# Moving the sums of ACT's partial products in a depthwise convolution from VectorE to GpSimd

## The chip, the cores and the metric

The kernel runs on one NeuronCore of a Trainium2 chip. The metric is the device time of one execution in microseconds, given as the median of several runs. A profile is taken of one further execution.

The engines are called by their names or by the short names of the profile: TensorE (PE, and PEld for its weight loads), VectorE (DVE), ScalarE (ACT), GpSimd (POOL) and SyncE (SP).

## The reference

A decoder trunk of two layers over 256 tokens of 2048 features, all in float32. Layer 0 mixes tokens with a Conformer convolution module, layer 1 with differential attention. Each layer goes on with a gated feed-forward part (5632 hidden features, a depthwise convolution of width 3) and a gated per-layer embedding. The change touches only the first mixer, of which this is the core:

```python
def conformer_conv(x, w_pw1, b_pw1, w_dw, b_dw, ln_g, ln_b, w_pw2, b_pw2):
    a, g = jnp.split(x @ w_pw1 + b_pw1, 2, axis=-1)
    u = a * jax.nn.sigmoid(g)
    u = causal_dwconv(u, w_dw) + b_dw          # 31 taps for each feature
    u = jax.nn.silu(layer_norm(u, ln_g, ln_b))
    return u @ w_pw2 + b_pw2
```

## The kernel before

**Tiling.** Features lie on the 128 partitions, so the 2048 features are 16 feature tiles, and the 256 tokens are the columns. The first mixer works on one feature tile at a time (the code counts `p` from 0 to 15, `PAIRS` is 16). All engines run their own instruction streams, written out by hand; they meet only at counting semaphores.

**What each engine does for a tile p of the first mixer.**

- TensorE computes two blocks of `x @ w_pw1` into PSUM, the value block and the gate block of the tile (`glu_unit`, matmul at L1783). It may run up to four tiles ahead of VectorE, since it has PSUM banks for two chunks of two tiles.
- ACT computes the sigmoid of the gate block (`gate_of`, L747). VectorE multiplies it with the value block into `u_ext` (`gated`, L1213). `u_ext` holds 30 columns of zeros and then the 256 tokens, so that a tap is a shifted view of it.
- The 31 taps are shared out. ACT takes taps 0 to 9 (`first_taps`, L768, `ACT_PAIRS` is 5): the first two begin the accumulators `acc2` (from the third tile on ACT does only tap 0 of these and VectorE tap 1), the other eight are written as four products `products[:, 0..3]`, each with two halves of 256 columns, 512 columns in all. VectorE takes taps 10 to 30 (`convolve`, L1237), each a multiply-add into one of the two halves of `acc2`. For the last tile TensorE takes the last 14 taps as matmuls with diagonal matrices (`tap_diag`, L1876), and VectorE only eight.
- The four products must become one. In `convolve`, VectorE adds `products[:, 1]`, `[:, 2]` and `[:, 3]` onto `products[:, 0]`, three sums of 128x512, spread between its taps (L1248). Each waits for its product (`products_made`) and for the sum before it (`products_added`). `join` (L1255) adds the result to `acc2`, and L1261 adds its two halves into `vq`. ACT squares that (L755), and `add_up` (L1224) keeps the running sum over tiles for the layer norm.

`join(p)` is not called at once but behind `gated(p + 1)`, so that ACT can start the next tile's taps early. ACT may overwrite a product of the tile before only when `products_added` has counted the sum that read it.

**Behind the last tile.** TensorE takes the token means of the values and the squares, VectorE centres, scales and splits them, GpSimd computes a reciprocal root on two columns (`power`, L566), and the second pointwise matmul begins. From there on the kernel streams weights: SP loads blocks of 256 KB, ACT rounds each into `w_hi`, VectorE computes the remainder `w_lo`, and TensorE multiplies with both.

**GpSimd** makes constants, issues a few DMAs and computes the reciprocal roots. Its queue in the first mixer holds `load_gain` and `load_bias` (two DMAs, at 42 us), and then the root of the layer norm.

Of the kernel before, what the change touches and what calls it, by code (L numbers as in the profile page):

```python
# [24 lines left out]
ALU = mybir.AluOpType  # L25
# [42 lines left out]
def trunk(nc, t, out):  # L68
# [20 lines left out]
    ACT_PAIRS = 5  # L89
# [5 lines left out]
    PAIRS = 2 * CH_GLU  # L95
# [107 lines left out]
    def tenant(at, name, shape, dt=F32):  # L203
        assert at % 32 == 0
        return nc.alloc_sbuf_tensor_at(name, shape, dt, offset=at)
# [23 lines left out]
    products = tenant(arena + 16 * SLOT, "products", [P, ACT_PAIRS - 1, 2, T])  # L229
# [35 lines left out]
    with ctx:  # L265
        def sem(name):
            return ctx.enter_context(nc.semaphore(name))
# [46 lines left out]
        products_made = sem("products_made")  # L314
        products_added = sem("products_added")
# [107 lines left out]
        def load_constants(engine, which):  # L423

            n = 0
            for g, (parts, _, _, _) in enumerate(groups):
                row = 0
                for _, src in parts:
                    if consts_loader(n) == which:
                        engine.dma_start(const_rows[row:row + src.shape[0], g], src).then_inc(consts_landed[which], 16)  # L430
                    row += src.shape[0]
                    n += 1
# [113 lines left out]
        def _(pool):  # L546
# [15 lines left out]
            def power(dst, src, n):  # L562

                powers[0] += 1
                pool.wait_ge(var_ready, powers[0])
                nc.gpsimd.tensor_tensor(dst, src, minus_half[:, 0:n], ALU.pow).then_inc(rstd_ready, 1)  # L566
# [5 lines left out]
            def load_bias(src):  # L572
                pool.dma_start(bias[:], src.partition_broadcast(P)).then_inc(bias_landed, 16)
# [4 lines left out]
            load_gain(t["post_mix_g"][0])  # L578
            pool.wait_ge(cols_turned, len(groups))
            load_bias(t["conv_b_pw2"][0])  # L580
            power(rstd[:], meansq[:], HALVES)
            pool.wait_ge(early_ready, EARLY[0])
            pool.dma_start(z_saved[0][:], z_early[:]).then_inc(early_stored, 16)
# [41 lines left out]
        def _(act):  # L625
# [92 lines left out]
            def keep_columns(some):  # L718
                for g in some:
                    _, rows, of, first = groups[g]  # L720
                    act.wait_ge(cols_turned, g + 1 if g < 2 else len(groups))
                    dst = {"cols": cols, "conv": wconv}[of]
                    bank, at = column_bank(g)
                    nc.scalar.copy(dst[:, first:first + rows], ps[:, bank, at:at + rows]).then_inc(cols_ready, 1)
# [307 lines left out]
        def _(dve):  # L1032
# [183 lines left out]
            def add_up(p):  # L1216

                if 1 <= p < SUMMED:
                    dve.wait_ge(squared, p + 1)
                    if p == SUMMED - 1:  # L1220
                        dve.wait_ge(v_done, p + 1)
                    if p > 1:
                        dve.wait_ge(v_summed, p - 1)
                    nc.vector.tensor_tensor(vq_sum[:], vq[:, p], vq[:, 0] if p == 1 else vq_sum[:], ALU.add).then_inc(v_summed, 1)  # L1224

            def convolve(p, taps):

                both, sums = acc2[:, p % 2], products[:, 0]
                dve.wait_ge(glu_done, p + 1)
                dve.wait_ge(accs_begun, p + 1)  # L1230
                made = [None, None]
                each = len(taps) // (ACT_PAIRS - 1)
                for n, tap in enumerate(taps):
                    a = n % 2
                    if made[a] is not None:
                        dve.wait_ge(dve_step, made[a])
                    step.mark(nc.vector.scalar_tensor_tensor(both[:, a], u_ext[:, p, tap:tap + T],  # L1237
                                                             wconv[:, tap * KT + p:tap * KT + p + 1],
                                                             nshift[:] if tap == 1 else both[:, a], ALU.mult, ALU.add))
                    made[a] = step.value()  # L1240
                    if p == PAIRS - 2 and n == len(taps) // 2:
                        add_up(p - 1)
                    k = (n + 1) // each
                    if (n + 1) % each == 0 and 1 <= k < ACT_PAIRS - 1:
                        dve.wait_ge(products_made, (ACT_PAIRS - 1) * p + k + 1)
                        if k > 1:
                            dve.wait_ge(products_added, (ACT_PAIRS - 1) * p + k - 1)
                        nc.vector.tensor_tensor(sums, sums, products[:, k], ALU.add).then_inc(products_added, 1)  # L1248
                dve.wait_ge(dve_step, step.value())
                dve.wait_ge(products_added, (ACT_PAIRS - 1) * p + ACT_PAIRS - 2)  # L1250
# [12 lines left out]
            for p in range(PAIRS):  # L1263
                if p == 1:
                    unscaled(1)
                gated(p)
                if p:
                    join(p - 1)
                if p == 2:
                    dve.wait_ge(shift_ready, 1)  # L1270
                    dve.wait_ge(v_done, 2)
                    nc.vector.tensor_tensor(vq[:, 0:2, 0], vq[:, 0:2, 0], nshift[:].unsqueeze(1).to_broadcast([P, 2, T]),
                                            ALU.add).then_inc(v_shifted, 1)
                if 3 <= p < PAIRS - 1:
                    add_up(p - 2)
                taps = list(range(2 * ACT_PAIRS, CK - (PE_TAPS if p == PAIRS - 1 else 0)))
                convolve(p, taps if p < 2 else taps[0:1] + [1] + taps[1:])
                if p == PAIRS - 3:
                    split(None, 0, 0, 1)
# [87 lines left out]
            for layer in range(DEPTH):  # L1367
                if layer == 1:
# [83 lines left out]
                    for a in range(STEPS):  # L1452
# [7 lines left out]
                        c, k = divmod(a - PV_LAG - 1, BPC)  # L1460
# [627 lines left out]
```

## Time and profile before

| | us |
|---|---|
| median of 3 runs | 2421.08 |
| lowest and highest run | 2413.65, 2421.11 |
| the profiled execution | 2422.17 |
| its span | 2420.4 |
| TensorE busy | 2410.6 (100%) |
| VectorE busy | 1640.4 (68%) |
| ACT busy | 1239.0 (51%) |
| GpSimd busy | 36.2 (1%) |

The span runs from the first to the last recorded instruction; 1.8 us of the profiled execution lie outside it. Busy shares are means over the whole span, and a busy TensorE is not TensorE at its peak, because matmuls overlap and their ends are modelled. A float32 matmul leaves two records. The first mixer ends near 346 us; its convolution, of which the change is a part, lies between 35 and 246 us.

### The profile page before, as it was taken

The page shows a single profiled execution, that of the slowest core. Times are in us where ns is not written, and L with a number is a line of the kernel's source. Part 1 is how long each engine was busy: PE and PEld are TensorE (multiplying, and loading weights), DVE is VectorE, ACT ScalarE, POOL GpSimd, SP SyncE. Part 2 cuts the span into 40 slices and gives each one's busy share as a digit, 9 for nine tenths or more (in the row PEclk, how much of TensorE's full clock was granted, in tenths as well). Part 3 has the DMA queues.
Part 4 walks back from the last instruction along what each step waited for, and adds up shares of the span by engine and source line. Part 5 has one row for each costly group of instructions (what it writes and reads, how often), then busy time and mean ns, then how long its engine had stood idle before and what let it go on. Part 6 is the DMA issues. An engine that isn't in the chain of part 4 may idle for free.

```text
span 2420.4 us, 38834 instructions
## 1 busy us (share of the span) xinstructions
PE 2410.6 (100%) x12378; PEld 2058.2 (85%) x12378; DVE 1640.4 (68%) x2231; ACT 1239.0 (51%) x1777; POOL 36.2 (1%) x66
## 2 busy tenths in 40 slices
PE   9999999999999999999999999999999999999999
PEld 8888788888888888888888888888888888888887
DVE  6999767777777754447655677577777777644475
ACT  3433655555555544446644455466655656544464
POOL 2000000000000000000000000000000000000000
PEclk9999999999999999999999999999999999999999
DMA  8552546656656565556566544645566566655564
GB/s 265 180 166 92 174 157 197 183 180 193 184 177 198 183 211 193 195 193 221 193 202 206 182 157 150 196 157 182 184 199 190 182 191 194 210 193 194 193 231 150
DMA packets 370942, 452.48 MB, mean 187 GB/s; under 512 B 27460, under 2 KB 279494, under 8 KB 369440
## 3 DMA queue, kind: packets, MB, share of 16 engines
q1 hardware_dynamic: 367456, 435.54, 56.5%
q0 software_dynamic: 2960, 15.02, 1.8%
q8 instruction: 44, 0.72, 0.1%
q10 hardware_dynamic: 432, 0.79, 0.1%
q14 instruction: 50, 0.41, 0.1%
HBM read 447.05 MB, written 4.19 MB: 186 GB/s over the span
## 4 chain that ended last, share of the span: by engine, by line
PE 98%; SPq 0%; DVE 0%; issue 0%; DMA 0%; ACT 0%; POOL 0%; DVEq 0%; POOLq 0%; ACTq 0%
PE ps L1701 32%; PE ps L1703 16%; PE ps L1728 13%; PE ps L1730 13%; PE ps L1729 13%; PE ps L1783 9%; PE ps L1673 1%; PE ps L1949 0%; PE ps L1935 0%; SPq L477 0%; DMA h<-in_x 0%; PE ps L1876 0%; PE ps L1790 0%; PE ps L1884 0%; PE ps L1657 0%
## 5 line engine op out<-in xcount | busy, mean ns | idle before, releaser
L1044 DVE TENSOR_TENSOR w_lo<-raw,w_hi 128x1024 fp32r<-128x1024 f32 x758 | 923.8, 1224 | 631.8 <-ACT w_hi L634 625.7
L1701 PE MATMUL ps<-x,w_hi 128*128 128x512 f32 x3328 | 1165.5, 396 | 1.3 <-DVE w_lo L1044 1.3
L634 ACT CAST w_hi<-raw 128x1024 fp32r<-128x1024 f32 x758 | 791.4, 1049 | 727.7 <-PE ps L1730 361.8
L1703 PE MATMUL ps<-x,w_lo 128*128 128x256 f32 x3328 | 928.7, 279 | 0.0
L1701 PEld LDWEIGHTS ps<-x,w_hi 128*128 128x128 f32 x3328 | 624.4, 188 | 149.3 <-DVE w_lo L1044 1.8
L1703 PEld LDWEIGHTS ps<-x,w_lo 128*128 128x128 f32 x3328 | 627.1, 188 | 0.0
L1728 PE MATMUL ps<-w_hi,mid 128*128 128x512 f32 x704 | 273.9, 389 | 0.0
L1729 PE MATMUL ps<-w_lo,mid 128*128 128x512 f32 x704 | 273.9, 389 | 0.0
L1730 PE MATMUL ps<-w_hi,mid 128*128 128x512 f32 x704 | 273.9, 389 | 0.0
L1728 PE MATMUL ps<-w_hi,x 128*128 128x512 f32 x640 | 253.2, 396 | 0.0
L1730 PE MATMUL ps<-w_hi,x 128*128 128x512 f32 x640 | 249.2, 389 | 0.0
L1729 PE MATMUL ps<-w_lo,x 128*128 128x512 f32 x640 | 249.2, 389 | 0.0
L1783 PE MATMUL ps<-xn,wg 128*128 128x256 f32 x896 | 193.7, 379 | 0.0
L1783 PEld LDWEIGHTS ps<-xn,wg 128*128 128x128 f32 x896 | 170.2, 190 | 23.1
L1505 DVE SCALAR_TENSOR_TENSOR acc<-ext,cols,acc 128x256 f32<-128x256 f32 x352 | 147.2, 480 | 46.0 <-ACT acc L951 39.6
L1728 PEld LDWEIGHTS ps<-w_hi,mid 128*128 128x128 f32 x704 | 132.2, 188 | 27.5
L1730 PEld LDWEIGHTS ps<-w_hi,mid 128*128 128x128 f32 x704 | 132.2, 188 | 27.4
L1729 PEld LDWEIGHTS ps<-w_lo,mid 128*128 128x128 f32 x704 | 132.2, 188 | 27.4
L1730 PEld LDWEIGHTS ps<-w_hi,x 128*128 128x128 f32 x640 | 120.1, 188 | 25.4
L1728 PEld LDWEIGHTS ps<-w_hi,x 128*128 128x128 f32 x640 | 120.2, 188 | 24.8 <-issue 0.4
L1729 PEld LDWEIGHTS ps<-w_lo,x 128*128 128x128 f32 x640 | 120.2, 188 | 24.6 <-issue 0.2
L1237 DVE SCALAR_TENSOR_TENSOR acc<-u_ext,wconv,acc 128x256 f32<-128x256 f32 x322 | 134.1, 482 | 1.2 <-ACT acc L768 1.1
(202 smaller groups left out, 1310.4 us busy)
## 6 DMA issues: line engine op xcount, KB each, us to landing
raw<-in_ffn_w_in SPq DMA_DIRECT2D x704, 256.0 KB, 3.1
raw<-in_ffn_w_out SPq DMA_DIRECT2D x352, 256.0 KB, 3.5
raw<-in_attn_w_qkv SPq DMA_DIRECT2D x192, 256.0 KB, 2.9
raw<-in_ple_w_gate SPq DMA_DIRECT2D x128, 256.0 KB, 3.6
wg<-in_conv_w_pw SPq DMA_DIRECT2D x112, 256.0 KB, 4.0
raw<-in_conv_w_pw SPq DMA_DIRECT2D x64, 256.0 KB, 3.6
raw<-in_attn_w_o SPq DMA_DIRECT2D x64, 256.0 KB, 3.5
wg<-in_conv_w_pw SPq DMA_DIRECT2D x32, 128.0 KB, 4.0
```

The lines of the kernel that those rows point to most:

```text
L634: nc.scalar.copy(w_hi[:, u % RING], raw[:, u % RING]).then_inc(hi_split, 1)
L1044: nc.vector.tensor_tensor(w_lo[:, u % RING], raw[:, u % RING], w_hi[:, u % RING].bitcast(F32), ALU.subtract).then_inc(split_done, 1)
L1237: step.mark(nc.vector.scalar_tensor_tensor(both[:, a], u_ext[:, p, tap:tap + T], wconv[:, tap * KT + p:tap * KT + p + 1], nshift[:] if tap ...
L1505: ins = nc.vector.scalar_tensor_tensor(acc[:, f], ext[:, f, tap:tap + T], col(f"ffn_tap{layer}{tap}", c * 2 + (f if f < 2 else FT + f - 2) ...
L1673: ins = nc.tensor.transpose(tiles[:, turned_at(left, kt), P * half:P * (half + 1)], h[:, half, P * kt:P * (kt + 1)], ident[:])
L1701: mm(ps[:, 4 * s + f], w_hi[:, u % RING, q, columns], x[:, kt].rearrange("p a t -> p (a t)"), start=kt == 0, stop=False)
L1703: ins = mm(ps[:, 4 * s + f, 0:T], w_lo[:, u % RING, q, columns], x[:, kt, 0], start=False, stop=kt == KT - 1)
L1728: mm(bank(half), hi, w_hi[:, u % RING, q], start=first, stop=False)
L1729: mm(bank(half), hi, w_lo[:, u % RING, q], start=False, stop=False)
L1730: ins = mm(bank(half), lo, w_hi[:, u % RING, q], start=False, stop=last)
L1783: ins = mm(ps[:, 4 * (c % 2) + f, 0:T], wg[:, glu_slot(u), q, P * f:P * (f + 1)], source[:, kt], start=kt == 0, stop=kt == KT - 1)
```

## The change

The three sums of products for tiles 0 to 14 are written into GpSimd's stream, ahead of the root of the layer norm, with the same semaphores. VectorE keeps only those of tile 15. Its wait for the third sum at the end of `convolve` (`products_added` at 4p + 3) stays, and is now a wait for GpSimd. The sum is the same operation on the same columns: 128x512 float32, written in place onto `products[:, 0]`.

```diff
@@ -578,6 +578,12 @@
             load_gain(t["post_mix_g"][0])
             pool.wait_ge(cols_turned, len(groups))
             load_bias(t["conv_b_pw2"][0])
+            for p in range(PAIRS - 1):
+                for k in range(1, ACT_PAIRS - 1):
+                    pool.wait_ge(products_made, (ACT_PAIRS - 1) * p + k + 1)
+                    if k > 1:
+                        pool.wait_ge(products_added, (ACT_PAIRS - 1) * p + k - 1)
+                    nc.gpsimd.tensor_tensor(products[:, 0], products[:, 0], products[:, k], ALU.add).then_inc(products_added, 1)
             power(rstd[:], meansq[:], HALVES)
             pool.wait_ge(early_ready, EARLY[0])
             pool.dma_start(z_saved[0][:], z_early[:]).then_inc(early_stored, 16)
@@ -1241,7 +1247,7 @@
                     if p == PAIRS - 2 and n == len(taps) // 2:
                         add_up(p - 1)
                     k = (n + 1) // each
-                    if (n + 1) % each == 0 and 1 <= k < ACT_PAIRS - 1:
+                    if p == PAIRS - 1 and (n + 1) % each == 0 and 1 <= k < ACT_PAIRS - 1:
                         dve.wait_ge(products_made, (ACT_PAIRS - 1) * p + k + 1)
                         if k > 1:
                             dve.wait_ge(products_added, (ACT_PAIRS - 1) * p + k - 1)
```

VectorE's order for the fourth tile (p = 3) before, from its gated product to the next one. A name's number tells apart buffers of one name, and x5 means five in a row:

```order
L1213 SCALAR_TENSOR_TENSOR u_ext<-ps,cols,glu_gate 128x256
L1255 TENSOR_TENSOR acc_94<-acc_94,products 128x512
L1261 TENSOR_TENSOR vq<-acc_94 128x256
L1224 TENSOR_TENSOR vq_sum<-vq 128x512
L1237 SCALAR_TENSOR_TENSOR acc_94<-u_ext,wconv,acc_94 128x256
L1237 SCALAR_TENSOR_TENSOR acc_94<-u_ext,wconv,nshift 128x256
L1237 SCALAR_TENSOR_TENSOR acc_94<-u_ext,wconv,acc_94 128x256 x3
L1248 TENSOR_TENSOR products<-products 128x512
L1237 SCALAR_TENSOR_TENSOR acc_94<-u_ext,wconv,acc_94 128x256 x5
L1248 TENSOR_TENSOR products<-products 128x512
L1237 SCALAR_TENSOR_TENSOR acc_94<-u_ext,wconv,acc_94 128x256 x5
L1248 TENSOR_TENSOR products<-products 128x512
```

The same tile in the changed kernel, whose lines lie six further down:

```order
L1219 SCALAR_TENSOR_TENSOR u_ext<-ps,cols,glu_gate 128x256
L1261 TENSOR_TENSOR acc_94<-acc_94,products 128x512
L1267 TENSOR_TENSOR vq<-acc_94 128x256
L1230 TENSOR_TENSOR vq_sum<-vq 128x512
L1243 SCALAR_TENSOR_TENSOR acc_94<-u_ext,wconv,acc_94 128x256
L1243 SCALAR_TENSOR_TENSOR acc_94<-u_ext,wconv,nshift 128x256
L1243 SCALAR_TENSOR_TENSOR acc_94<-u_ext,wconv,acc_94 128x256 x20
```

The three sums between the taps are gone, and the taps stand in one row of 22. GpSimd's queue in the first mixer in the changed kernel, from the first root to the store behind the second:

```order
L566 TENSOR_TENSOR rstd<-meansq,minus_half 128x2
L570 DMA gain<-in_post_mix_g 128x2048
L573 DMA bias<-in_conv_b_pw 128x2048
L586 TENSOR_TENSOR products<-products 128x512 x45
L566 TENSOR_TENSOR rstd<-meansq,minus_half 128x2
L589 DMA z_saved<-z_early 128x2048
```

The row with x45 is new, three sums for each of 15 tiles; the other rows stand there as before. The streams of TensorE, ACT and SP are the same in both kernels.

## Rows read from the trace of the kernel before

**Rows 1.** The page: TensorE's busy time (first line), and the chain that ended last

```profile
PE 2410.6 (100%) x12378; PEld 2058.2 (85%) x12378; DVE 1640.4 (68%) x2231; ACT 1239.0 (51%) x1777; POOL 36.2 (1%) x66
...
PE 98%; SPq 0%; DVE 0%; issue 0%; DMA 0%; ACT 0%; POOL 0%; DVEq 0%; POOLq 0%; ACTq 0%
```

**Rows 2.** Busy us of PE, PEld, DVE, ACT, POOL; clock; DMA, by window

```profile
50.50:235.50 185.00, 185.00 (x859) 162.86 (x858) 175.28 (x403) 69.59 (x168) 0.00 (x0) 1.00 0.48 153
```

**Rows 3.** Timeline of VectorE: start us, us, engine, line, operation [idle before <-releaser]

```profile
98.56 0.48 DVE L1213 SCALAR_TENSOR_TENSOR u_ext<-ps,cols,glu_gate 128x256 f32<-128x256 f32 x1
...
102.60 0.69 DVE L1248 TENSOR_TENSOR products<-products 128x512 f32<-128x512 f32 x1
103.20 2.06 DVE L1237 SCALAR_TENSOR_TENSOR acc<-u_ext,wconv,acc 128x256 f32<-128x256 f32 x5
...
112.15 0.48 DVE L1213 SCALAR_TENSOR_TENSOR u_ext<-ps,cols,glu_gate 128x256 f32<-128x256 f32 x1 [0.93 <-ACT glu_gate L747]
```

**Rows 4.** Timeline of ACT: a tile's products, and the gates of the last two tiles

```profile
99.67 3.30 ACT L768 ACTIVATE products<-u_ext,wconv 128x256 f32<-128x256 f32 x8
...
222.05 0.47 ACT L747 ACTIVATE glu_gate<-ps,cols 128x256 f32<-128x256 f32 x1 [7.55 <-PE ps L1783]
...
235.87 0.47 ACT L747 ACTIVATE glu_gate<-ps,cols 128x256 f32<-128x256 f32 x1 [8.46 <-PE ps L1783]
```

**Rows 5.** VectorE's waits, 50 to 237 us: us, times, longest; and the last of them

```profile
DVE u_ext L1213 <- ACT glu_gate L747: 9.5, 9, 1.2
...
236.47 0.48 DVE L1213 SCALAR_TENSOR_TENSOR u_ext<-ps,cols,glu_gate 128x256 f32<-128x256 f32 x1 [0.53 <-ACT glu_gate L747]
```

**Rows 6.** Timeline of the last tile: TensorE's diagonal taps, and VectorE's use of them

```profile
237.01 5.02 PE L1876 MATMUL ps<-u_ext,tap_diag 128*128 128x256 f32 x22
...
243.10 1.54 PE L1876 MATMUL ps<-u_ext,tap_diag 128*128 128x256 f32 x6
...
244.75 0.42 DVE L1259 TENSOR_TENSOR acc<-ps,acc 128x256 f32<-128x256 f32 x1 [0.43 <-PE ps L1876]
```

**Rows 7.** Timeline of GpSimd, around the layer norm of the first mixer

```profile
247.85 0.72 POOL L566 TENSOR_TENSOR rstd<-meansq,minus_half 128x2 f32<-128x2 f32 x1 [204.42 <-DVE meansq L1310]
```

**Rows 8.** Groups of GpSimd instructions: busy us, mean ns of one, idle before

```profile
L597 POOL TENSOR_SCALAR_AFFINE_SELECT mask<-mask 128x128 f32<-128x128 f32 x1 | 0.5, 484 | 0.1
L594 POOL MEMSET mask<- 128x256 f32 x1 | 0.3, 332 | 0.0
...
L551 POOL MEMSET minus_half<- 128x16 f32 x1 | 0.1, 109 | 0.0
```

**Rows 9.** Timeline and groups: GpSimd instructions that overlap with VectorE's

```profile
1189.21 0.69 DVE L1083 TENSOR_TENSOR z<-z,gain 128x512 f32<-128x512 f32 x1
1189.39 1.06 POOL L566 TENSOR_TENSOR rstd<-meansq,minus_half 128x2 f32<-128x2 f32 x1 [75.30 <-DVE meansq L1062]
...
1482.39 1.01 POOL L566 TENSOR_TENSOR orstd<-omean,minus_half 128x4 f32<-128x4 f32 x1 [13.04 <-DVE omean L1440]
1482.44 1.23 DVE L1044 TENSOR_TENSOR w_lo<-raw,w_hi 128x1024 fp32r<-128x1024 f32 x1
...
1577.63 0.68 DVE L1085 TENSOR_TENSOR y_mix<-ps,gain 128x512 f32<-128x512 f32 x1
1577.80 0.70 POOL L566 TENSOR_TENSOR rstd<-meansq,minus_half 128x2 f32<-128x2 f32 x1 [85.74 <-DVE meansq L1062]
...
L566 POOL TENSOR_TENSOR orstd<-omean,minus_half 128x4 f32<-128x4 f32 x4 | 4.1, 1015 | 216.3 <-DVE omean L1440 216.3
```

**Rows 10.** Timeline of the first tile's end: VectorE's result, TensorE's load of it

```profile
49.52 0.42 DVE L1261 TENSOR_TENSOR vq<-acc 128x256 f32<-128x256 f32 x1
50.27 0.41 PEld L1838 LDWEIGHTS ps<-vq,inv_p 128*128 128x128 f32 x2
```

**Rows 11.** Timeline of TensorE: one small matmul at the program's start and later

```profile
1.54 2.93 PE L1790 MATMUL ps<-ident 128*128 128x128 f32 x12 [1.54 <-POOL minus_half L551]
...
347.40 1.06 PE L1790 MATMUL ps<-ident 128*128 128x128 f32 x8
```

## The prediction

> **What bounds the kernel now.** I read the page first: TensorE is busy for 2410.6 us of the 2420.4 us span, and the chain that ended last is 98% TensorE [rows 1]. So a saving on another engine is worth nothing unless TensorE waits for it, and a delay costs only where TensorE comes to wait.
>
> The change lies in the first mixer, so I next took the busy time of each engine in that stretch [rows 2]: from 50.5 to 235.5 us TensorE has 185.0 of 185.0 us at a granted clock of 1.00 (2.4 GHz), VectorE 175.28 us, GpSimd none. TensorE's pairs of matmul blocks (one feature tile each) set the pace, and VectorE, which convolves one tile per pair, follows with little to spare.
>
> How little is read in VectorE's timeline [rows 3]. The gated product of one tile starts at 98.56 us, the next at 112.15 us after 0.93 us of idling for ACT's gate. So a tile is 12.66 to 12.7 us of VectorE work, against 13.82 us between two gates, which is TensorE's pair (235.87 less 222.05) [rows 4]. The waits of the stretch sum it up: VectorE waited for a gate nine times, 9.5 us in all, the last time directly before the last tile, at 236.47 us [rows 5]. This **9.5 us is VectorE's whole reserve**. The first of the nine is at 112.15 us: until then it was behind TensorE. Work added beyond the reserve moves the last tile's start, one for one. Work taken away only lengthens the waits, since the last gate comes from TensorE at 235.87 us whatever VectorE does.
>
> What hangs on that start: TensorE's 14 diagonal taps of the last tile begin at 237.01 us, when the gated product is there, and VectorE adds their sum at 244.75 us before the normalization can begin [rows 6]. From there to the end the chain is TensorE's own, and nothing behind gives time back.
>
> **The change part by part.** *Removed from VectorE*: 45 sums over 128x512 (three for each of 15 tiles). One takes 0.69 us, but the next instruction starts 0.60 us behind it (102.60 to 103.20) [rows 3]. This is 45 x 0.60 = 27.0 us. By itself it is worth nothing at the end: the cover that hides VectorE, TensorE's own 185 us, is already the longer.
>
> *Added on GpSimd*: 45 sums of the same shape. The queue there is empty for 204 us before 247.85 us, where the reciprocal root of the normalization comes [rows 7]; both DMAs in the queue lie before that. ACT has a tile's products ready at 102.97 us (99.67 + 3.30), 4.4 us behind the start of the gated product, and VectorE wants the sum only behind its 22 taps, at 111.2 us (112.15 - 0.93) [rows 3, 4], so even three sums of 1.7 us are done in time and the new wait for them at the end of a tile is empty, if GpSimd may read when it likes. ACT overwrites a product only in the next tile, before which it idles for 8.46 us [rows 4].
>
> *Price of one GpSimd sum.* The trace has none of this size. The nearest rows [rows 8]: a memset of 16 columns took 109 ns and one of 256 columns 332 ns, so 0.93 ns for each column written and 0.09 us fixed; an affine select over 128 columns, which reads too, took 484 ns, 3.0 ns a column. With one pass of 512 columns at the memset's rate the low end is 0.57 us, at the select's rate the high end 1.6 us. I take two passes, one for each operand, at the memset's rate: 2 x 512 x 0.93 ns + 0.09 = 1.04 us. The memsets are the plainer work, while the select has to compare as well.
> By the Trainium skill (GPSIMD Engine Reference, 3.1 Elementwise — side-by-side cycle accounting) such an addition over 2048 columns takes 4497 ns, because both operands pass one read port; a quarter would be 1.12 us, an estimate from that page, and the sum below would end 3.6 us higher by it.
>
> *What that does to VectorE.* Here is the step on which everything rests. At 1189.39 us GpSimd's small root began while VectorE ran a product of two SBUF operands (z and gain, until 1189.90), and took 1.06 us. The same instruction at 1577.80 us, beside a product of which one operand is in PSUM, took 0.70 us [rows 9]. The 0.36 us more is about what was left of VectorE's instruction: the two do not read SBUF together. All 22 taps and the sums of a tile have two SBUF operands. So I expect the taps and the GpSimd sums to run one after the other, and each GpSimd sum to hold VectorE for its length, 1.04 us, where VectorE's own cost it 0.60.
> Against it stand 1482.39 and 1482.44 us [rows 9]: GpSimd began first, VectorE's two-operand subtraction right behind, and neither was longer than usual (1.01 us beside a mean of 1.015 over four such roots; 1.23 us for 1024 columns is no more than twice the 0.69 us of 512). I put this down to the size: four columns are read at once.
> The Trainium skill (SBUF — State Buffer, Who interferes with whom) gives whoever starts first the shared ports for the whole instruction, and by that the subtraction should have ended 0.9 us late. The trace does not agree in that pair, and agrees at 1189 us.
>
> *The sum.* Held for h per sum, VectorE gets 45 x (h - 0.60) more work, of which 9.5 us is absorbed. With h = 1.04: 19.8 - 9.5 = **10.3 us**. Check by tiles: 12.68 + 3 x 0.44 = 14.0 us a tile, above the 13.82 us of a pair, and at 98.56 us VectorE is late already, since it waits only a tile later; so VectorE never catches up and all of its waits go. The first tile also delays TensorE, whose means of that tile are loaded at 50.27 us, 0.33 us after VectorE's sum [rows 10]; that runs beside VectorE's own lag and adds nothing. TensorE itself, which may be four pairs ahead, goes on to 235.7 us and then stands.
>
> *Clock.* It will stand in two pieces of some 4 to 6 us, before the sum of squares and before the taps. At the program's start, after no work, 12 small matmul records took 2.93 us, 0.24 each; the same form later took 1.06 us for 8, so 0.13 or less each [rows 11], though the granted clock reads 1.00 in both. If the first ran at 1.2 instead of 2.4 GHz, the loss there was about 1.4 to 1.6 us. The taps and what follows are on the path, so I add 1.6 us. The ends are 0 and 6.6 us (all 28 tap records, 5.02 + 1.54 us, at half speed) [rows 6].
> The Trainium skill (TensorE: Matmul & The Clock Gate, Part 1) has the array fall to the lower level after idling, which no row of this trace shows inside the program.
>
> Total: 10.3 + 1.6 = 11.9 us. The profiled execution took 2422.2 us, so 2434.1; the median of the runs, 2421.1, lies 1.1 us below it: **2433.0 us**, 0.5% slower. About 0.3%, or 7.3 us, is what a measurement of this kernel can tell from no change.
>
> **The rivals.** *R1, no slower: the sums run beside the taps.* If GpSimd takes only gaps between VectorE's instructions, or h stays at or below 0.81 us (9.5 / 45 + 0.60, the point where the reserve is used up), the last gated product stays at 236.47 us and the time at 2421 us. For it: the undisturbed pair at 1482 us, and the low end of 0.57 us. Against it: 1189 us. Up to h = 0.97 the result is still within 0.3%, without the clock term. Chance 0.29.
>
> *R2, much slower.* If a sum holds VectorE for the 1.6 us of the select's rate, or if GpSimd is kept out while taps follow each other and does its three sums when VectorE has stopped, with a handover each, the addition is up to 45 x 1.0 - 9.5 = 35.5 us, with the clock 37: 2458 us. The middle of such cases is near 2445 us. For it: the taps start every 0.4 us and last 0.48, so there may be no gap at all. Against it: the root at 1189 us got in as soon as one instruction of VectorE ended. Chance 0.12.
>
> *R3, faster: VectorE's 27 us come off the path.* This wants TensorE to wait for VectorE in the stretch; it shows no idle time there [rows 2], and the 0.33 us at 50 us is on the good side. Chance 0.04. That the change doesn't do what it says I leave at nothing: the order of the instructions shows the 45 sums moved.
>
> **How the numbers follow.** The forecast, h from about 0.95 to 1.2 us, has 0.55 and its own range from 2427 to 2440 us (45 x 0.35 - 9.5 = 6.3; 45 x 0.60 - 9.5 = 17.5, with up to 1.6 more). Slower by over 0.3% is the forecast and R2: 0.67. Within it is R1: 0.29. Faster: 0.04. A range that holds 8 in 10 must take in R1, so it begins at 2420 us, and it ends at 2445 us, which leaves out half of R2 and R3.
>
> **What would show it.** Right: GpSimd has 45 instructions of 128x512 of over 1 us between 37 and 245 us; taps that follow a start of one are stretched or late by up to a microsecond; VectorE's waits for the gate are gone after 112 us; the last gated product comes near 247 us in place of 236.47; TensorE idles from 236 us; from the normalization on, each stage is as long as before. The clock term is right if the 22 tap records take over 5.02 us. Wrong: taps every 0.40 us beside a running GpSimd sum and longer waits for the gate (R1), or a wait of VectorE for GpSimd at the end of each tile (R2).

## The result, and the profile after

| | before | after |
|---|---|---|
| median of 20 runs each, us | 2417.18 | 2434.34 |
| lowest and highest | 2412.05, 2430.95 | 2424.83, 2443.98 |
| the profiled execution | 2422.17 | 2443.98 |
| its span | 2420.4 | 2442.2 |
| VectorE busy | 1640.4 | 1655.4 |
| GpSimd busy | 36.2 | 98.4 |

The change makes the kernel slower: the ratio is 1.0059, with a 95% interval from 1.0044 to 1.0073. The prediction was 2433.0 us against 2421.1.

The runs of either kernel stand on steps 9 us apart: before near 2412, 2421 and 2431 us, after near 2425, 2434 and 2443. Step by step the difference is about 13 us. Half of the twenty runs before lie at or below 2413.65 us and the next is at 2420.71, so the median of 2417.18 stands between two steps, where no run is. The two profiled executions stand on different steps, so their difference, 21.8 us, is not the price of the change. GpSimd's timeline shows both parts. First the three marks of the kernel before (start us, us, engine, line, operation, idle before): the root of the layer norm has its row ahead of the prediction [rows 7], at 247.85 us, and these are the two loads of a gain behind the large matmul stages of the two feed-forward parts.

```profile
863.40 0.55 POOL L570 DMA_DIRECT2D gain<-in_post_ffn_g  x1 [494.06 <-DVE mid L1527]
...
2089.10 0.60 POOL L570 DMA_DIRECT2D gain<-in_post_ffn_g  x1 [492.06 <-DVE mid L1527]
```

The same in the changed kernel:

```profile
260.91 0.72 POOL L566 TENSOR_TENSOR rstd<-meansq,minus_half 128x2 f32<-128x2 f32 x1 [21.38 <-DVE meansq L1316]
...
876.36 0.56 POOL L570 DMA_DIRECT2D gain<-in_post_ffn_g  x1 [494.05 <-DVE mid L1533]
...
2110.86 0.60 POOL L570 DMA_DIRECT2D gain<-in_post_ffn_g  x1 [501.00 <-DVE mid L1533]
```

At the root the changed kernel is 13.06 us late, at 876 us 12.96 us. Then the wait in front of the last row is 501.00 us in place of 492.06, and the distance is 21.76. The waits in front of these two rows took 485.1 or 494.1 us, and 492.1 or 501.0 us, in the profiles of all the kernels shown here, in any combination, with or without work on GpSimd in the first mixer. This is a variation of the large stages, not of the change. So **the start of the variance instruction that precedes the root (247.61 us before, 260.67 us after) is the measure used below.** Behind it, the distance between the two profiles changes by 0.1 us up to each of these rows, but for these stages.

The start of the program varies too. The first gated product of the mixer, which lies ahead of everything that the change touches, starts 0.42 us earlier in the profile of the changed kernel; before and after:

```profile
35.20 0.48 DVE L1213 SCALAR_TENSOR_TENSOR u_ext<-glu,cols,glu_gate 128x256 f32<-128x256 f32 x1 [0.54 <-ACT glu_gate L747]
...
34.78 0.49 DVE L1219 SCALAR_TENSOR_TENSOR u_ext<-glu,cols,glu_gate 128x256 f32<-128x256 f32 x1 [0.55 <-ACT glu_gate L753]
```

Counted from there, the changed kernel is 13.48 us late at the variance instruction, not 13.06.

Where this time lies is shown by the busy times of the changed kernel (columns as in [rows 2]):

```profile
50.50:235.50 185.00, 183.23 (x849) 161.35 (x850) 183.80 (x344) 69.57 (x169) 53.13 (x40) 1.00 0.47 152
235.50:255.00 19.50, 12.56 (x44) 10.35 (x43) 18.51 (x36) 6.17 (x15) 3.74 (x3) 0.74 0.01 2
```

VectorE has 59 instructions fewer than in [rows 2], yet is busy for 183.80 us in place of 175.28. In the second stretch TensorE works for 12.56 of 19.50 us and its granted clock is 0.74 on average. The chain that ended last, 98% TensorE before [rows 1], now goes through VectorE for 8%:

```profile
PE 90%; DVE 8%; issue 1%; SPq 0%; DMA 0%; POOL 0%; ACT 0%; DVEq 0%; POOLq 0%; ACTq 0%
```

How a GpSimd sum meets the taps is seen in the timeline of VectorE and GpSimd in one tile:

```profile
108.61 0.48 DVE L1243 SCALAR_TENSOR_TENSOR acc<-u_ext,wconv,acc 128x256 f32<-128x256 f32 x1
108.66 1.56 POOL L586 TENSOR_TENSOR products<-products 128x512 f32<-128x512 f32 x1 [9.55 <-ACT products L774]
109.00 1.50 DVE L1243 SCALAR_TENSOR_TENSOR acc<-u_ext,wconv,acc 128x256 f32<-128x256 f32 x1
110.36 1.26 POOL L586 TENSOR_TENSOR products<-products 128x512 f32<-128x512 f32 x1
110.42 1.48 DVE L1243 SCALAR_TENSOR_TENSOR acc<-u_ext,wconv,acc 128x256 f32<-128x256 f32 x1
111.83 0.47 DVE L1243 SCALAR_TENSOR_TENSOR acc<-u_ext,wconv,acc 128x256 f32<-128x256 f32 x1
```

The first sum comes 0.05 us behind the start of a tap, and takes 1.56 us in place of 1.27: it waits for that tap. The tap after it lasts 1.50 us in place of 0.48. So it goes with each sum: one tap is 1.02 us late, and the next starts 1.42 us behind it in place of 0.40. VectorE's own sum cost it 0.60 us.

The first tile is another matter. Its sums could begin only behind GpSimd's two DMAs, the first of which waits for TensorE; the timeline of GpSimd and VectorE:

```profile
41.89 0.59 POOL L570 DMA_DIRECT2D gain<-in_post_mix_g  x1 [18.67 <-PE ps L1789]
42.48 0.53 POOL L573 DMA_DIRECT2D bias<-in_conv_b_pw  x1
43.03 5.71 POOL L586 TENSOR_TENSOR products<-products 128x512 f32<-128x512 f32 x3
49.25 0.76 DVE L1202 TENSOR_TENSOR glu<-ps,rstd_all 128x256 f32<-128x256 f32 x2 [4.44 <-issue]
```

VectorE has finished the tile's taps at 44.8 us and idles for 4.44 us for the third sum. The second gated product comes at 50.58 us, where it came at 48.40; counted from the first one it is 2.60 us late.

The last tile, as in [rows 5, 6]:

```profile
246.78 0.48 DVE L1219 SCALAR_TENSOR_TENSOR u_ext<-ps,cols,glu_gate 128x256 f32<-128x256 f32 x1
247.32 7.77 PE L1882 MATMUL ps<-u_ext,tap_diag 128*128 128x256 f32 x22 [1.70 <-DVE u_ext L1219]
256.17 1.54 PE L1882 MATMUL ps<-u_ext,tap_diag 128*128 128x256 f32 x6
257.82 0.42 DVE L1265 TENSOR_TENSOR acc<-ps,acc 128x256 f32<-128x256 f32 x1 [3.19 <-PE ps L1882]
```

The gated product is 10.31 us late by the two profiles, 10.73 us counted from the first one, without a wait in front of it. The 22 tap records take 7.77 us in place of 5.02, which is 2.75 us. 10.73 + 2.75 = 13.48: the whole shift.

### The profile page after: what moved, and what is told of

Same layout as the page of the kernel before. It is cut to its first block, busy times and chain, and to the rows that moved or that the text cites. A ratio compares the mean times of both kernels' runs of the same rounds, so it can differ in the third digit from the quotient of the medians.

```text
span 2442.2 us, 38834 instructions
## 1 busy us (share of the span) xinstructions
PE 2423.7 (99%) x12378; PEld 2065.3 (85%) x12378; DVE 1655.4 (68%) x2186; ACT 1237.8 (51%) x1777; POOL 98.4 (4%) x111
## 4 chain that ended last, share of the span: by engine, by line
PE 90%; DVE 8%; issue 1%; SPq 0%; DMA 0%; POOL 0%; ACT 0%; DVEq 0%; POOLq 0%; ACTq 0%
PE ps L1707 32%; PE ps L1709 16%; PE ps L1734 13%; PE ps L1735 13%; PE ps L1736 13%; DVE acc L1243 7%; PE ps L1789 1%; PE ps L1679 1%; PE ps L1955 0%; PE ps L1941 0%; PE ps L1882 0%; DVE vq_sum L1230 0%; DVE acc L1261 0%; SPq L477 0%; DVE u_ext L1219 0%
## 5 line engine op out<-in xcount | busy, mean ns | idle before, releaser
L1243 DVE SCALAR_TENSOR_TENSOR acc<-u_ext,wconv,acc 128x256 f32<-128x256 f32 x322 | 172.9, 606 | 1.2 <-ACT acc L774 1.1
L1735 PEld LDWEIGHTS ps<-w_lo,mid 128*128 128x128 f32 x704 | 132.1, 188 | 27.2
```

The source lines that it names most:

```text
L1735: mm(bank(half), hi, w_lo[:, u % RING, q], start=False, stop=False)
```

## The experiments

Theory A is the prediction's: a GpSimd instruction that reads SBUF keeps VectorE's two-operand instructions from reading meanwhile, and what exceeds VectorE's reserve of 9.5 us moves the last tile. The rivals: any GpSimd activity does it (B), the loss comes from the new waits between engines (C), VectorE's sums were on the path (D). "The marker" is the variance instruction. The start of the program differs by up to 1.2 us from one profile to another, as the first gated product of the mixer shows; so the two columns of "later" count from there, and compare with the kernel before. All times are in us.

| kernel | first gated product | last gated product | marker | last, later by | marker, later by | 22 tap records |
|---|---|---|---|---|---|---|
| before | 35.20 | 236.47 | 247.61 | | | 5.02 |
| the change | 34.78 | 246.78 | 260.67 | 10.73 | 13.48 | 7.77 |
| only writing | 34.77 | 236.04 | 247.18 | 0.00 | 0.00 | 5.02 |
| one operand read | 34.02 | 241.59 | 255.22 | 6.30 | 8.79 | 7.51 |
| two operands, apart | 34.45 | 272.89 | 286.26 | 37.17 | 39.40 | 7.25 |
| half the columns | 34.42 | 248.53 | 261.96 | 12.84 | 15.13 | 7.31 |
| the sums left out | 34.70 | 235.98 | 247.12 | 0.01 | 0.01 | 5.02 |
| one sum of three | 34.01 | 235.75 | 246.89 | 0.47 | 0.47 | 5.02 |
| DMAs behind the first tile | 34.35 | 245.04 | 258.96 | 9.42 | 12.20 | 7.80 |
| DMAs in the seventh tile | 34.33 | 246.01 | 259.08 | 10.41 | 12.34 | 6.96 |
| TensorE kept busy | 34.58 | 246.60 | 257.74 | 10.75 | 10.75 | 5.02 |

The experiments with a ratio have nine or ten executions, the others the profiled one alone.

### GpSimd busy, but only writing

```diff
+            for p in range(PAIRS - 1):
+                for k in range(1, ACT_PAIRS - 1):
+                    pool.wait_ge(products_made, (ACT_PAIRS - 1) * p + k + 1)
+                    for _ in range(2):
+                        ...
+                        nc.gpsimd.memset(scratch[:], 0.0).then_inc(scratch_made, 1)
```

> The kernel before (VectorE keeps all its sums), with 90 GpSimd memsets of 128x512 on spare memory, two at each place where the change has a sum, so GpSimd is as busy as in the change but reads nothing. The marker is the start of the variance instruction of the layer norm: 247.6 us before, 260.7 us in the change. Theory A (a GpSimd sum keeps VectorE's two-operand taps from reading): taps stay 0.40 us apart and 0.48 us long, VectorE waits 9.5 us for gates, marker 247.6 us. Rival B (any GpSimd activity holds VectorE for its length, 0.57 us a memset): 90 x 0.57 - 9.5 = 42 us more, marker near 290 us. Rival C (the loss comes from the new waits between the engines, not from sharing) also 247.6 us.

The group of the memsets and VectorE's group of taps, in this kernel (busy us, mean ns, idle before):

```profile
L591 POOL MEMSET scratch<- 128x512 f32 x90 | 47.3, 526 | 138.4 <-ACT products L781 132.2
...
L1250 DVE SCALAR_TENSOR_TENSOR acc<-u_ext,wconv,acc 128x256 f32<-128x256 f32 x322 | 133.8, 476 | 1.2 <-ACT acc L781 1.1
```

The marker is at 247.18 us, no later than before when counted from the first gated product. The taps take 476 ns (482 before), and the one execution took 2412.74 us, the lowest step of the kernel before. 47 us of GpSimd work cost nothing: B falls.

### One operand read

In the place of the two memsets; the inner loop now runs once:

```diff
+                        nc.gpsimd.tensor_scalar(scratch[:], h[:, 0, 0:512], 2.0, None, ALU.mult).then_inc(scratch_made, 1)
```

> As the run before, with 45 GpSimd multiplications by a constant, 128x512 from one SBUF operand onto spare memory. Theory A with a hold for as long as GpSimd reads: one operand is half the reading of a sum, so a tap beside it comes about 0.5 us late in place of 1.02 us, 45 x 0.5 - 9.5 = 13 us, marker 260 us, with the slower clock 263 us. If only two-operand instructions on GpSimd collide, 247.6 us. If one operand holds as long as two, 45 x 1.02 - 9.5 = 36.4 us, marker 284 us or, with the clock, 287 us. Rival C: 247.6 us.

The timeline of VectorE and GpSimd around one of them:

```profile
105.23 1.78 POOL L591 TENSOR_SCALAR scratch<-h 128x512 f32<-128x512 f32 x1 [7.29 <-ACT products L781]
105.58 0.83 DVE L1250 SCALAR_TENSOR_TENSOR acc<-u_ext,wconv,acc 128x256 f32<-128x256 f32 x1
106.33 0.47 DVE L1250 SCALAR_TENSOR_TENSOR acc<-u_ext,wconv,acc 128x256 f32<-128x256 f32 x1
```

The marker is at 255.22 us, the last gated product at 241.59. None of the three expectations was met in size: a tap is 0.35 us late, not 0.5, though the instruction itself runs for 1.78 us (1.49 us where it has nothing to wait for), longer than a sum of two operands. 45 x 0.35 - 9.5 = 6.3 us, and 6.30 us are found, counted from the first gated product. What holds VectorE is therefore not the length of the GpSimd instruction but a part of it: the held tap ends at 106.41 us and the next one runs untouched, while GpSimd is at work until 107.01. In a sum of two operands the part is three times as long. That it is the reading is inferred: this run differs from the next in the operation as well as in the operands.

### Two operands read, and no one waits for the sum

```diff
+                        nc.gpsimd.tensor_tensor(scratch[:], h[:, 0, 0:512], h[:, 1, 0:512], ALU.add).then_inc(scratch_made, 1)
```

> As the run before, with 45 GpSimd sums of two SBUF operands, 128x512, onto spare memory. VectorE keeps its own 45 sums and waits for GpSimd nowhere. Theory A: each sum delays one tap by 1.02 us, 45 x 1.02 - 9.5 = 36.4 us more until the last gated product, and 2.7 us for TensorE's lower clock behind its waits: marker 286.7 us, whole execution about 39 us longer than before. Rival C (waits and dependencies): 247.6 us, no change.

The last gated product, TensorE's taps and the variance in the timeline:

```profile
272.89 0.48 DVE L1226 SCALAR_TENSOR_TENSOR u_ext<-ps,cols,glu_gate 128x256 f32<-128x256 f32 x1
273.43 7.25 PE L1889 MATMUL ps<-u_ext,tap_diag 128*128 128x256 f32 x22 [2.30 <-DVE u_ext L1226]
286.26 0.16 DVE L1323 SCALAR_TENSOR_TENSOR meansq<-ps,ssum 128x2 f32<-128x2 f32 x1
```

The last gated product is 36.42 us late by the profiles where 36.4 were expected, and the marker is at 286.26 where 286.7 was. Counted from the first gated product it is 37.17 us; that the first number meets the forecast so closely is luck. Part of the 0.8 us more is that 12 of the 45 GpSimd sums met one of VectorE's own sums in place of a tap, and held it for about 1.06 us. The execution took 2460.74 us, 39.2 us above the median of 13 runs of the kernel before on the same chip (2421.52); the marker is 39.40 us later. VectorE reads nothing that GpSimd writes here and waits for it nowhere, so C falls as the cause of the bulk.

### The same over half the columns

```diff
-                        nc.gpsimd.tensor_tensor(scratch[:], h[:, 0, 0:512], h[:, 1, 0:512], ALU.add).then_inc(scratch_made, 1)
+                        nc.gpsimd.tensor_tensor(scratch[:, 0:256], h[:, 0, 0:256], h[:, 1, 0:256], ALU.add).then_inc(scratch_made, 1)
```

> The kernel before, with 45 GpSimd sums of two SBUF operands, but over 128x256 in place of 128x512, onto spare memory; VectorE keeps its own sums. If a tap is held for as long as GpSimd reads, two operands by 256 columns hold it about half of 1.02 us, 0.5 us, 45 x 0.5 - 9.5 = 13 us, the last gated product near 249.5 us and the marker near 263 us with the lower clock. If each sum costs a fixed handover, 1.02 us whatever its size, the marker comes at 286 us.

The timeline of GpSimd and VectorE at the second sum:

```profile
44.61 0.73 POOL L591 TENSOR_TENSOR scratch<-h 128x256 f32<-128x256 f32 x1
44.67 0.95 DVE L1250 SCALAR_TENSOR_TENSOR acc<-u_ext,wconv,acc 128x256 f32<-128x256 f32 x1
```

In this timeline a tap of 0.95 us is 0.48 us late; the last gated product is at 248.53 us, the marker at 261.96. Counted from the first gated product the last is 12.84 us late, where 13 were expected. The hold goes with the columns: 1.02 us for 512, 0.48 for 256, so 2.1 ns a column. The rival of a fixed handover falls.

### The sums left out

```diff
-                        nc.vector.tensor_tensor(sums, sums, products[:, k], ALU.add).then_inc(products_added, 1)
+                        if p < PAIRS - 1:
+                            dve.sem_inc(products_added, 1)
+                        else:
+                            nc.vector.tensor_tensor(sums, sums, products[:, k], ALU.add).then_inc(products_added, 1)
```

> The kernel before without its 45 sums of products in tiles 0 to 14 (they are left out, so three of four products of those tiles are missing from the result); the semaphore counts are kept. It bounds what moving them away could give at best. Theory A: VectorE only waits longer for its gates, 9.5 + 27.0 = 36 us less what it had not caught up, marker 247.6 us, time as before within 0.1%. Rival D (VectorE's sums were on the path): up to 27 us faster.

VectorE's waits from 50 to 237 us in this kernel (us in total, times, longest), to be read beside [rows 5]:

```profile
DVE u_ext L1213 <- ACT glu_gate L747: 36.7, 14, 3.0
```

VectorE waits for 36.7 us in place of 9.5, which is the 27.2 us of its sums, and the marker stays where it was, 0.01 us later when counted from the first gated product. The ratio of the times is 1.0011 (0.9989 to 1.0034). The best that could come of moving the sums away is nothing: D falls.

### One sum of three on GpSimd

```diff
-                for k in range(1, ACT_PAIRS - 1):
+                for k in range(1, 2):
...
-                    if p == PAIRS - 1 and (n + 1) % each == 0 and 1 <= k < ACT_PAIRS - 1:
+                    if (n + 1) % each == 0 and (1 if p == PAIRS - 1 else 2) <= k < ACT_PAIRS - 1:
```

The two DMAs also stand behind the first tile's sum, as in the next experiment.

> The change, with only the first of the three sums of each tile on GpSimd, VectorE keeps the other two, and GpSimd's two DMAs stand behind the first tile's sum. Theory A: 15 x (1.02 - 0.60) = 6.3 us more work for VectorE, less than its reserve of 9.5 us, so the last gated product stays at 236.5 us, the marker at 247.6 us, and the time as before within 0.1%; about 3 us of VectorE's waits for gates are left. If each use of GpSimd cost the path something, about a third of the change's 13 us, 4 us, would show.

VectorE's waits from 50 to 237 us, the last gate, and the last gated product, which has no wait in front of it:

```profile
DVE u_ext L1220 <- ACT glu_gate L754: 3.6, 5, 0.7
...
234.82 0.47 ACT L754 ACTIVATE glu_gate<-ps,cols 128x256 f32<-128x256 f32 x1 [8.05 <-PE ps L1790]
...
235.75 0.48 DVE L1220 SCALAR_TENSOR_TENSOR u_ext<-ps,cols,glu_gate 128x256 f32<-128x256 f32 x1
```

3.6 us of waits are left, and the ratio is 0.9996 (0.9980 to 1.0013). The price of about 4 us is not there. Yet the last gated product is 0.47 us later, counted from the first one, although waits are left. The last gate itself comes 0.14 us later. The other 0.33 us is VectorE's: in the kernel before it has only 0.53 us of waiting behind 208.84 us [rows 5], since a weight remainder stands in its queue ahead of the last but one gated product:

```profile
221.54 1.23 DVE L1044 TENSOR_TENSOR w_lo<-raw,w_hi 128x1024 fp32r<-128x1024 f32 x1
```

The sums of two tiles on GpSimd cost 2 x 0.42 = 0.84 us there. So the reserve is not one sum to draw on: what was waited earlier doesn't help the last tiles as long as VectorE still waits in between.

### The DMAs behind the first tile's sums

```diff
-            pool.wait_ge(glu_used, UPC)
-            load_gain(t["post_mix_g"][0])
-            pool.wait_ge(cols_turned, len(groups))
-            load_bias(t["conv_b_pw2"][0])
             for p in range(PAIRS - 1):
+                if p == 1:
+                    pool.wait_ge(glu_used, UPC)
+                    load_gain(t["post_mix_g"][0])
+                    pool.wait_ge(cols_turned, len(groups))
+                    load_bias(t["conv_b_pw2"][0])
```

> The change, with GpSimd's two DMAs (gain and bias, which wait for TensorE until 41.9 us) moved behind the first tile's three sums. In the change these sums begin only at 43.03 us and VectorE waits 4.44 us for the last. Theory A: the wait goes, three holds of 1.02 us come in its place, so the second gated product comes 1.4 us earlier (49.2 us) and the marker is near 259.3 us. On the first sum, which took 2.89 us where others take 1.27: if it is the first use of the instruction, it takes 2.89 us again and no tap is stretched in its first 1.6 us; if it was kept out by VectorE's taps, it now varies.

The timeline of GpSimd and VectorE at the very first sum:

```profile
37.54 1.27 POOL L587 TENSOR_TENSOR products<-products 128x512 f32<-128x512 f32 x1 [14.76 <-ACT products L775]
37.56 1.53 DVE L1244 SCALAR_TENSOR_TENSOR acc<-u_ext,wconv,acc 128x256 f32<-128x256 f32 x1
```

In this timeline the first sum starts at 37.54 us, takes 1.27 us and holds a tap at once, so its 2.89 us in the change were not the price of a first use. The wait of 4.44 us is gone, the second gated product is at 48.81 us, the marker at 258.96 (259.3 expected). The ratio to the kernel before is 1.0052 (1.0035 to 1.0069). Counted from the first gated product, the second one comes 1.34 us earlier than in the change (1.4 expected) and the marker 1.28 us. The queue's order is worth 1.3 us of the 13.5.

### The DMAs between two sums of the seventh tile

```diff
             for p in range(PAIRS - 1):
                 for k in range(1, ACT_PAIRS - 1):
+                    if p == 6 and k == 2:
+                        pool.wait_ge(glu_used, UPC)
+                        load_gain(t["post_mix_g"][0])
+                        pool.wait_ge(cols_turned, len(groups))
+                        load_bias(t["conv_b_pw2"][0])
```

> The change, with GpSimd's two DMAs (gain, bias) moved between the first and the second sum of the seventh tile, in the midst of VectorE's taps. Open is why the very first sum of the change took 2.89 us, 1.6 us of them without holding a tap: it began directly behind the second DMA issue, and it ended its wait as VectorE's taps ran out. Theory E (GpSimd is still at work on the DMA it has issued): the second sum of the seventh tile takes some 2.9 us, no tap is stretched in its first 1.6 us, and all other sums take 1.27 to 1.56 us. Theory F (VectorE's taps kept it out): that sum takes 1.27 to 1.56 us and stretches the tap beside its start. Under both the marker is near that of the kernel with the DMAs behind the first tile's sums, 259 us, since the tile has time for a late sum.

The timeline of GpSimd and VectorE in the seventh tile:

```profile
122.29 0.59 POOL L570 DMA_DIRECT2D gain<-in_post_mix_g  x1
122.55 2.45 DVE L1244 SCALAR_TENSOR_TENSOR acc<-u_ext,wconv,acc 128x256 f32<-128x256 f32 x1
122.88 0.54 POOL L573 DMA_DIRECT2D bias<-in_conv_b_pw  x1
123.43 1.28 POOL L587 TENSOR_TENSOR products<-products 128x512 f32<-128x512 f32 x1
```

Theory E is out here: the sum right behind the DMAs takes 1.28 us. That is as theory F had it, but F did not foresee what the timeline shows: the tap that started ahead of the sum, while GpSimd was issuing the first DMA, was held until the sum was nearly over, 1.97 us in all. The marker is at 259.08 us where 259 was expected, and that is luck: the last gated product is 0.99 us later than in the experiment before (by the table), and the taps of the last tile take 6.96 us in place of 7.80. Why the first sum of the change waited 1.6 us while four taps went by at their usual pace stays open. In the three kernels with reading instructions apart, the first one waited too (2.54 us with one operand; 2.32 us with two over 512 columns, 1.79 over 256), until VectorE changed from one of its own sums to a tap.

### TensorE kept busy while it waits

```diff
             pe.wait_ge(glu_done, PAIRS - 1)
+            keep_warm(22, 6)
             pe.wait_ge(v_summed, SUMMED - 1)
             mean_of(vq_sum, 0)
             token_means(vq_sum, ((0, 0), (1, 3)), 0)
+            keep_warm(8, 6)
             pe.wait_ge(glu_done, PAIRS)
```

> The change, with 22 and 8 small matmuls (identity by identity, not used) in the two places where TensorE waits ahead of the last tile's taps. If the low granted clock there (0.74 from 235.5 to 255 us) costs what I read, the 22 tap records take 5.0 us again in place of 7.8, the clock reads 1.00 and the marker comes at 257.9 us, 2.75 us earlier than in the change; the last gated product stays at 246.8 us. If the taps were long for another reason (reading beside other engines), the marker stays at 260.7 us.

The taps of the last tile and the stretch around them:

```profile
247.14 5.02 PE L1884 MATMUL ps<-u_ext,tap_diag 128*128 128x256 f32 x22 [1.11 <-DVE u_ext L1219]
...
235.50:255.00 19.50, 17.91 (x118) 16.09 (x116) 18.44 (x36) 5.97 (x15) 3.56 (x3) 1.00 0.00 1
```

The last gated product is where it was (246.60 us; 10.75 us late where the change was 10.73), the clock is 1.00, the taps take 5.02 us and the marker is at 257.74 us (257.9 expected). The ratio to the kernel before is 1.0046 (1.0029 to 1.0063). The clock term is shown: these are the 2.75 us.

## Why the prediction was right

- **The bound.** Held. TensorE's pace sets the stretch; leaving the sums out gave nothing. The reserve of 9.5 us held for the change, because all the waits were used up. It is not the reserve of a smaller load: one sum of three added 6.3 us and already cost 0.47.
- **The price of a sum.** The prediction took 1.04 us for the sum and for the hold. The hold is 1.02 us, but the sum takes 1.27 us (median of 45), so the number was right for the hold and 0.23 us too low for the instruction. That they met at the hold is partly luck: the two passes at the memset's rate were a guess, and a memset of 512 columns took 0.53 us. From 256 to 512 columns the trace has 0.73 to 1.27 us, 2.1 ns a column and 0.2 us fixed. The figure of the Trainium skill (GPSIMD Engine Reference, 3.1 Elementwise — side-by-side cycle accounting), 4497 ns for 2048 columns, agrees with that line, which gives 4.5 us there, an estimate; only its quarter, 1.12 us, is too low, since it divides the fixed part too.
- **One after the other.** Held, tap by tap. No experiment varied VectorE's operands. One sign for the condition of two SBUF operands is in the run with one operand read: at 46.91 us a GpSimd multiplication began, and VectorE's product with one operand in PSUM at 46.93 us took 0.41 us, as before. The doubt at 1482 us, where a root over four columns held nothing, fits what the hold follows: one operand of 512 columns holds 0.35 us, two of 256 hold 0.48, two of 512 hold 1.02, a memset nothing. Four columns would be some ten nanoseconds, an estimate from the 2.1 ns a column.
- **The sum.** 10.3 us predicted, 10.73 measured at the last gated product (10.31 if the start of the program is left in; that this is the predicted number is luck), with one term wrong inside. The step that failed is "both DMAs in the queue lie before that", and with it "the new wait for them at the end of a tile is empty". It holds for 14 tiles. In the first one the DMA ahead waits for TensorE until 41.89 us, the sums come late and VectorE waits 4.44 us. Counted anew: 42 sums x 0.42 us = 17.6 us; the first tile 2.6 us, where the formula had 3 x 0.44 = 1.3; less 9.5: 10.7 us. The 1.3 us too little there and the 0.02 us too much on each of the other sums, 0.8 us in all, cancel for the most part. TensorE waited 2.04 us for the first tile's result; as the prediction says, that ran beside VectorE's lag.
- **The clock.** 1.6 us predicted from the slow first matmuls of the program, 2.75 us measured. The mechanism was right, the size too small by 1.15 us. TensorE stood for 5.24 and 1.70 us, where the prediction had two pieces of 4 to 6. The price is not a constant: in the six kernels whose taps ran slower, the 22 records lost between 1.94 and 2.78 us.
- **Total.** 11.9 us predicted, 13.5 measured in the profiles; by the medians of 20 runs 17.2 us, and by the ratio 14.3 us (0.0059 x 2417, from 10.6 to 17.6 by its interval), since medians also move with the steps of 9 us.
- **The rivals.** R1 needed a hold of at most 0.81 us; it is 1.02. R2 needed GpSimd to be kept out until a tile's taps ran out; that happened once, to the first sum. R3 falls with the sums left out.

No version here beats the kernel before. Moving the sums off VectorE cannot gain anything here, because VectorE is not the bound.

## What to carry to other kernels

Before moving work off an engine, ask whether anyone waits for it: a run with the work simply left out prices the best case, here zero. An elementwise sum given to GpSimd beside two-operand work of VectorE took 1.02 us of VectorE's time here (512 columns, two float32 operands), which is more than VectorE needs for it (0.60). Compare the total with the receiver's and the neighbour's reserve, tile by tile behind the last wait and not only as one sum over the stage. Count from an event ahead of the change, since the start of the program moved by up to 1.2 us between profiles. And read what stands ahead in the queue that receives the work.

## What the runs showed of the hardware

- The hold depends on what GpSimd does with its operands, not on how long it runs: nothing for writing alone, and 0.35 us of an instruction that ran for 1.78 us. The Trainium skill (SBUF — State Buffer, SBUF: two separate sides) says that whoever starts first, a VectorE instruction with two SBUF inputs or a GpSimd one that reads SBUF, has the shared ports for the whole instruction. Here VectorE went on 0.6 us before the GpSimd instruction ended, so the hold is a part of it, presumably the reading. That a memset does not collide with a two-operand instruction agrees with the same page (Who interferes with whom).
- A multiplication by a constant over one operand took GpSimd 1.49 us at the least for 128x512 and 1.76 us on average, waits for VectorE's taps included. The sum of two operands took 1.26 us at the least and 1.38 on average.
- A VectorE tap was held for 1.97 us by a GpSimd queue in which two DMA issues and a sum followed each other, though no GpSimd instruction but the two DMA issues was running in the first 0.9 us. This was seen once; around the same DMAs at 42 us the taps went by at their usual pace.
- GpSimd's waits over the large stages of the feed-forward parts take one of two durations, 9 us apart (485.1 or 494.1, and 492.1 or 501.0 us), at a granted clock of 1.00 from 300 to 2400 us in every profile. What decides it was not studied.
- Behind waits of 5.24 and 1.70 us, with 2.7 us of work between them, TensorE's granted clock was down: 0.74 on average from 235.5 to 255 us, a mix of the levels 2.4 and 1.2 GHz.
